# Two DMA queues in the sample attention, later splits, and prompt heads taken in pairs

## The reference, cut to what matters

```
c_kv = rmsnorm(kv[:256]);  k_rope = rope(rmsnorm(kv[256:]))       # 256-wide latent, 32-wide rotary key
kvb  = c_kv @ w_kv_b                                              # 16 heads x (64 key + 64 value)
k_nope = rmsnorm(kvb[..., :64]) ;  v = kvb[..., 64:]
s = (q_nope . k_nope + q_rope . k_rope) * 96**-0.5                # per head
p = softmax(where(k_pos//64 <= q_pos//64, s, -inf))
o = p @ v                                                         # then o @ w_o
```

## Time and profile before

| | us |
|---|---|
| median of 3 runs (1977.75 to 1983.08) | 1980.14 |
| the profiled execution, its own time | 1976.72 |
| its span | 1974.8 |

### The profile page before, as it was taken

One profiled execution on the slowest core, in us unless ns is written; L12 is line 12 of the kernel. 1 busy time (PEld: TensorE's weight loads), 2 busy tenths in 40 slices (PEclk: granted clock), 3 DMA queues, 4 the chain that ended last, 5 costly groups with the idle time before them and its releaser, 6 DMA issues.

```text
span 1974.8 us, 28317 instructions
## 1 busy us (share of the span) xinstructions
PE 1876.7 (95%) x10584; PEld 1765.5 (89%) x10584; DVE 1144.0 (58%) x1733; ACT 827.3 (42%) x1427; POOL 245.5 (12%) x315
## 2 busy tenths in 40 slices
PE   9999998999998999999999999999996799999997
PEld 8999998788887999999999999866775589999997
DVE  6555448778878655545855544456665555555444
ACT  5333335555464433334533333355453334333233
POOL 1000111220220000011300001140022222000020
PEclk9999999999999999999999999999998999999999
DMA  5444444455352544444344444421033433444441
GB/s 196 127 127 128 139 148 145 138 177 204 107 181 88 179 127 126 129 132 135 116 132 124 127 139 139 158 66 32 33 102 92 128 104 118 126 125 125 138 137 64
DMA packets 67779, 249.71 MB, mean 126 GB/s; under 512 B 9480, under 2 KB 10760, under 8 KB 66416
## 3 DMA queue, kind: packets, MB, share of 16 engines
q1 hardware_dynamic: 54000, 196.67, 32.4%
q0 software_dynamic: 13696, 51.90, 8.3%
HBM read 235.74 MB, written 12.12 MB: 126 GB/s over the span
## 4 chain that ended last, share of the span: by engine, by line
PE 81%; DVE 9%; ACT 5%; issue 2%; DMA 2%; POOL 1%; SPq 0%; ACTq 0%; DVEq 0%; POOLq 0%
PE pair L1753 23%; PE pair L1755 23%; PE pair L1754 23%; DMA kn<-rs_rows 2%; DVE wlo L1143 1%; PE pair L2169 1%; PE pair L1760 1%; PE pair L1762 1%; PE pair L1761 1%; PE pair L1950 1%; ACT kn L1012 1%; ACT seg L803 1%; PE pair L1969 1%; PE pair L2171 1%; PE pair L2170 1%
## 5 line engine op out<-in xcount | busy, mean ns | idle before, releaser
L1753 PE MATMUL pair<-xh,whi 128*128 128x384 f32 x1960 | 664.0, 339 | 14.8 <-DVE xl L1153 12.6
L1754 PE MATMUL pair<-xl,whi 128*128 128x384 f32 x1960 | 657.7, 336 | 0.0
L1755 PE MATMUL pair<-xh,wlo 128*128 128x384 f32 x1960 | 657.6, 336 | 0.0
L1143 DVE TENSOR_TENSOR wlo<-raw,whi 128x1024 fp32r<-128x1024 f32 (+3 forms) x372 | 463.1, 1246 | 181.3 <-ACT whi L674 172.5
L674 ACT ACTIVATE whi<-raw 128x1024 fp32r<-128x1024 f32 (+2 forms) x369 | 379.0, 1029 | 296.7 <-PE pair L1755 282.5
L1753 PEld LDWEIGHTS pair<-xh,whi 128*128 128x128 f32 x1960 | 370.3, 189 | 25.4 <-issue 14.2
L1754 PEld LDWEIGHTS pair<-xl,whi 128*128 128x128 f32 x1960 | 370.1, 189 | 1.8 <-issue 1.2
L1755 PEld LDWEIGHTS pair<-xh,wlo 128*128 128x128 f32 x1960 | 369.9, 189 | 0.0
L1163 DVE TENSOR_TENSOR tg<-pair,rstd 128x384 f32<-128x384 f32 x88 | 49.0, 557 | 331.2 <-PE pair L1755 330.6
L1753 PE MATMUL pair<-ah,whi 128*128 128x384 f32 x704 | 237.0, 337 | 3.5 <-DVE tu L1164 3.3
L1754 PE MATMUL pair<-al,whi 128*128 128x384 f32 x704 | 236.6, 336 | 0.0
(11 more groups left out here) (400 smaller groups left out, 2295.0 us busy)
## 6 DMA issues: line engine op xcount, KB each, us to landing
raw<-in_stream SPq DMA_DIRECT2D x372, 512.0 KB, 3.6
S<-in_ssm POOLq DMA_DIRECT2D x4, 2048.0 KB, 9.2
out_ssm_s<-S POOLq DMA_DIRECT2D x4, 2048.0 KB, 8.0
seg<-acs_rows POOLq DMA_DIRECT2D x12, 512.0 KB, 5.1
cTb<-in_cacheT POOLq DMA_DIRECT2D x10, 512.0 KB, 4.0
kn<-rs_rows POOLq DMA_DIRECT2D x16, 264.0 KB, 5.6
lowC<-in_cache POOLq DMA_DIRECT2D x8, 512.0 KB, 5.5
lowA<-in_cacheT POOLq DMA_DIRECT2D x6, 512.0 KB, 3.9
```

The lines of the kernel that those rows point to most:

```text
L1143: V.tensor_tensor(wlo[:, r, 0:w], raw[:, r, 0:w], whi[:, r, 0:w].bitcast(F32), ALU.subtract).then_inc(lo_ready, 1)
L1753: M(out, whi[:, r, ws], mh_(k), start=first and k == k0, stop=False)
L1754: M(out, whi[:, r, ws], ml_(k), start=False, stop=False)
L1755: ins = M(out, wlo[:, r, ws], mh_(k), start=False, stop=last and k == k1 - 1)
```

## The change

1. SP takes over the norm rows and the value transfers. Its weight loop is cut at block `WO + SLOTS`; between its two parts it issues `rstd_rows(u)` (the `kn` transfers) and `past_values(b)`, and POOL keeps the latent and rotary rows of the next stream.
2. `keys_split(b+2)` moves from even to odd u on ACT and DVE; on ACT it now stands ahead of `s_latent` and `s_exp(u+1)`. `keys_split(1)` stands ahead of `s_exp(0)` on ACT.
3. The prompt loop runs over 8 pairs y. Two score products, four expansions, six transposes in a row (bank 6 and bank 2), two expansions, six value products that alternate between the two heads, that is between the lower and upper half of the output partitions, then two expansions. `PT` has two slots. ACT and DVE are reordered to match; the low part of the next latent stands behind the pair's output.
4. Absorption uses banks 0, 1, 6, 7; the turn of the last key norms goes to bank 2 behind step 3, the first sample scores behind step 5.

```diff
-            with sp.Fori(1, NBLK // SLOTS) as i:
...
+            def rstd_rows(u):
+                if u >= 2:
+                    sp.wait_ge(s_added, u - 1)
+                sp.dma_start(kn[:, u % 2, 0:KEYS], rs_spread(u)).then_inc(rk_ld[u % 2], 16)
+            def past_values(b):
+                sp.wait_ge(po_ps, MH + 2 * max(b - 1, 0))
...
+            cut = WO + SLOTS
+            blocks(1, cut // SLOTS)
...
+            for u in range(2, UNITS):
...
+                rstd_rows(u)
+                if u % 2 and u >= 4:
+                    past_values(u // 2)
...
# POOL
-            for u in range(2, UNITS):
-                b = u // 2
...
-                past_rstd_rows(u)
-                if u % 2 == 0 and b + 2 < STREAMS:
-                    past_keys(b + 2)
-                    past_rope(b + 2)
-                if u % 2 and b >= 2:
-                    past_values(b)
+            for b in range(2, STREAMS):
+                past_keys(b)
+                past_rope(b)
# ACT, prompt loop
+            for y in range(MH // 2):
+                for i in range(3):
+                    past_square(8 * y + i)
+                p_turned(2 * y)
+                p_turned(2 * y + 1)
...
+                past_square(8 * y + 3)
+                if y + 1 < MH // 2:
+                    p_exp(2 * y + 2)
+                past_square(8 * y + 4)
+                if y + 1 < MH // 2:
+                    p_exp(2 * y + 3)
...
+                past_square(8 * y + 5)
+                act.wait_ge(po_ps, 2 * y + 2)
+                A(xh[:, y, 0:SEQ], bank[7 if y % 2 else 3][:, 0:SEQ], ACT.Copy).then_inc(oh_ready, 1)
+                if 2 <= y + 1 < STREAMS:
+                    past_split(y + 1)
+                past_square(8 * y + 6)
...
# ACT, sample loop
+            keys_split(1)
             s_exp(0)
-            keys_split(1)
             for u in range(UNITS):
+                if u % 2 and u // 2 + 2 < STREAMS:
+                    keys_split(u // 2 + 2)
                 if u >= 2:
                     s_latent(u - 2)
                 if u + 1 < UNITS:
                     s_exp(u + 1)
                 s_turned(u)
-                if u % 2 == 0 and 2 <= u // 2 + 2 < STREAMS:
-                    keys_split(u // 2 + 2)
# DVE, prompt loop
+                for i in range(8):
+                    past_sums(8 * y + i)
+                    if i == 2 and more:
+                        p_max(2 * y + 2)
+                    if i == 3 and more:
+                        p_max(2 * y + 3)
+                    if i == 5:
+                        if more:
+                            p_norm(2 * y + 2)
...
+                        if 2 <= y + 1 < STREAMS:
+                            past_split(y + 1)
+                    if i == 6 and more:
+                        p_norm(2 * y + 3)
# PE, prompt loop
+                for i in range(4):
+                    past_expand(8 * y + i)
...
+                for x in (2 * y, 2 * y + 1):
+                    pe.wait_ge(p_ready, x + 1)
+                    for j in range(3):
+                        ins = nc.tensor.transpose(bank[2 if x % 2 else 6][:, tiles(j)], Pb[:, x % 2, tiles(j)], ident[:, :])
+                    ins.then_inc(pt_ps, 1)
+                past_expand(8 * y + 4)
+                past_expand(8 * y + 5)
+                pe.wait_ge(pt_ev, 2 * y + 2)
...
+                for k, q, at in ((0, 0, 0), (0, 1, 1), (1, 1, 2)):
+                    for e in range(2):
+                        x = 2 * y + e
+                        ins = M(out[VH * e:VH * e + VH, tiles(q)], Vp[:, k, VH * x:VH * x + VH], PT[:, e, tiles(at)],
...
+                past_expand(8 * y + 6)
+                past_expand(8 * y + 7)
# PE, absorption
+            for j in range(4):
+                absorb(j)
+            pe.wait_ge(past_rstd, 4)
+            rs_turn(bank[2], 6, 8)
+            absorb(4)
+            absorb(5)
...
             s_scores(0)
+            absorb(6)
+            absorb(7)
```

More of the change, by code:

```diff
@@ L399, in build @@
         UNITS = 2 * STREAMS
+        QC_BANK = (0, 1, 6, 7)
         CRED = SLOTS
@@ L468, in _, with blocks, one_block @@
                 sp.dma_start(raw[:, r, :], T["stream"][r]).then_inc(raw_loaded[r], 16)
-            with sp.Fori(1, NBLK // SLOTS) as i:
-                for r in range(SLOTS):
-                    sp.wait_ge(lo_ready, i * SLOTS + (r - SLOTS + 1))
-                    sp.dma_start(raw[:, r, :], T["stream"][i * SLOTS + r]).then_inc(raw_loaded[r], 16)
+            def blocks(i0, i1):
+                with sp.Fori(i0, i1) as i:
+                    for r in range(SLOTS):
+                        sp.wait_ge(lo_ready, i * SLOTS + (r - SLOTS + 1))
+                        sp.dma_start(raw[:, r, :], T["stream"][i * SLOTS + r]).then_inc(raw_loaded[r], 16)
+            def one_block(n):
+                sp.wait_ge(lo_ready, n - SLOTS + 1)
+                sp.dma_start(raw[:, n % SLOTS, :], T["stream"][n]).then_inc(raw_loaded[n % SLOTS], 16)
+            def rstd_rows(u):
[4 more added lines that the diff above has]
+                sp.wait_ge(po_ps, MH + 2 * max(b - 1, 0))
+                sp.dma_start(cnat[:, b % 2], T["cache"][b]).then_inc(cn_ld[b % 2], 16)
+                sp.dma_start(vnew[0:STEPS, b % 2, :], ckv[STEPS * b:STEPS * b + STEPS, 2, :]).then_inc(cn_ld[b % 2], 16)
+            cut = WO + SLOTS
+            blocks(1, cut // SLOTS)
+            for n in range(cut // SLOTS * SLOTS, cut):
+                one_block(n)
+            sp.wait_ge(rs_st, 16 * 3)
+            sp.wait_ge(past_sum, 8 * STREAMS)
+            rstd_rows(0)
+            rstd_rows(1)
+            sp.wait_ge(filled, 6)
+            past_values(0)
+            past_values(1)
+            for u in range(2, UNITS):
+                if u == 12:
+                    sp.wait_ge(rs_st, 16 * 5)
+                rstd_rows(u)
+                if u % 2 and u >= 4:
+                    past_values(u // 2)
+            for n in range(cut, -(-cut // SLOTS) * SLOTS):
+                one_block(n)
+            blocks(-(-cut // SLOTS), NBLK // SLOTS)
         @block.gpsimd
@@ L1022, in _, with p_turned @@
             past_split(1)
+            def p_turned(x):
+                act.wait_ge(pt_ps, x + 1)
+                A(PT[:, x % 2, :], bank[2 if x % 2 else 6][:, 0:384], ACT.Copy).then_inc(pt_ev, 1)
             p_exp(0)
[L1024 to L1042, removed]
+            p_exp(1)
+            for y in range(MH // 2):
[3 more added lines that the diff above has]
+                p_turned(2 * y + 1)
+                if y == 0:
+                    A(rsT2[0:MH, P:2 * P], bank[2][0:MH, 384:512], ACT.Copy).then_inc(rs_ev, 1)
+                past_square(8 * y + 3)
[4 more added lines that the diff above has]
+                    p_exp(2 * y + 3)
+                else:
                     act.wait_ge(rs_turn_ps, 2)
@@ L1045, in _ @@
                     A(rsT2[0:6 * MH, 0:P], bank[2][0:6 * MH, 3 * P:4 * P], ACT.Copy).then_inc(rs_ev, 1)
[L1046 to L1052, removed]
+                past_square(8 * y + 5)
[4 more added lines that the diff above has]
+                past_square(8 * y + 6)
+                if y in (1, 2):
+                    z = (xh, xl)[y - 1]
+                    act.wait_ge(q_kept, 12)
+                    A(z[NOPE:QD, :, SEQ:TOK], Qs[NOPE:QD, 4 * y - 4:4 * y, :, :].rearrange("p b h q -> p (b h q)").rearrange(
+                        "p (k c) -> p k c", k=KD), ACT.Copy).then_inc(stack_hi, 1)
+                past_square(8 * y + 7)
+                if y == MH // 2 - 2:
+                    act.wait_ge(past_sum, 48)
+                    A(ksq[:, :, 0:6], ksq[:, :, 0:6], ACT.Sqrt, bias=EPS, scale=1.0 / NOPE).then_inc(past_std, 1)
             def keys_split(b):
@@ L1652, in _, with p_norm @@
             dve.wait_ge(mask_ld, 16)
-            p_max(0)
-            for x in range(MH):
+            def p_norm(x):
                 s, o = x % 2, 48 + 8 * (x % 2)
-                if x + 1 < MH:
-                    p_max(x + 1)
                 dve.wait_ge(p_exp_ready, x + 1)
@@ L1661, in _ @@
                 V.tensor_scalar(Pb[:, s, 128:384], Pb[:, s, 128:384], sm[:, o + 7:o + 8], None, ALU.mult).then_inc(p_ready, 1)
[L1662 to L1666, removed]
+            p_max(0)
+            p_max(1)
+            p_norm(0)
+            p_norm(1)
+            for y in range(MH // 2):
+                more = y + 1 < MH // 2
+                for i in range(8):
[7 more added lines that the diff above has]
+                            p_norm(2 * y + 2)
+                        dve.wait_ge(oh_ready, y + 1)
+                        V.tensor_tensor(xl[:, y, 0:SEQ], bank[7 if y % 2 else 3][:, 0:SEQ], xh[:, y, 0:SEQ].bitcast(F32),
+                                        ALU.subtract).then_inc(ol_ready, 1)
+                        if 2 <= y + 1 < STREAMS:
+                            past_split(y + 1)
+                    if i == 6 and more:
+                        p_norm(2 * y + 3)
```

(34 more changed lines are left out.)

58 lines of the change are left out of this document (14 added, 44 removed).

## The result

The changed kernel takes 1929.39 us (median, 1928.1 to 1929.83), the kernel before beside it 1981.61; the ratio is 0.9739, interval 0.9719 to 0.976. The prediction was 1932. The profiled execution took 1929.40 with a span of 1927.6.

The account below looks back on a forecast made before the run. It took PE to bound the prompt loop nearly fully and a ring over DVE, POOL and a DMA the sample loop. Gains 15.1 + 1.1 + 1.6 + 1.9 + 28.2 = 47.9 us gave 1932; own range 1923 to 1941, whole 1919 to 1953.

Parts of the forecast that it names:

- The bound of the sample loop: Units 1 to 13: without late transfers DVE's 8.97 us per two units; 9.6 taken, 28.2 us gained.
- the same ring: Sample loop: a ring over DVE, POOL and a DMA bound it, 14.3 us for a stream's two units.
- The prompt loop: Prompt heads: a pair takes 14.95 us in place of 16.84, 15.1 us gained, bounds 0 to 17.
- The restart of 0.27 behind transposes: Prompt loop: the first expansion behind a transpose takes 0.50, a restart of 0.27 us; the change drops one.
- Side by side: Rival, prompt loop: value products of different halves overlap, 6.4 us more gained, 1926 us; chance 0.15.
- the forecast's serial term (1.46): Prompt loop: a pair's six value products run one after the other, 0.80 us a head less a slow start of 0.14.
- Landings take over: Rival, sample loop: late `craw` or rotary rows make a pair landing + 3.1, 16.2 us gained, 1944 us; chance 0.18.
- The prompt ring: Rival, prompt loop: the chain overshoots its 0.5 us of room, a pair takes 16.4, 1944 us; chance 0.12.
- the slower rival: Rival, sample loop: SP serves norm rows slowly; at a landing of 20 us, 23.5 lost, 2004 us; chance 0.03.
- the third sign: Prompt loop: the forecast is wrong if PE waits for `past_lo` at the start of a pair; no size given.
- The entry: Way into the sample loop: 1.1 us gained before absorption, 1.6 from there to unit 0, 1.9 to unit 1.
- The untouched code: Rest of the kernel, outside the prompt loop, entry and sample loop: 0 us gained.

Follow-up runs that it names:

- e2: Kernel before with only the norm rows and value transfers moved to SP, splits still at even units: 1968.91 us, ratio 0.9925.
- e3: Kernel before with only the splits moved to odd units and the first ahead of the first exponential, transfers still on POOL: 1991.95 us, ratio 1.0043.
- e11: Changed kernel with a pair's six transposes taken apart (three, an expansion, three, an expansion): 1925.35 us.
- e1: Changed kernel with the six value products of a pair issued head by head, not alternating: 1931.08 us.
- e9: Changed kernel measured once more, unchanged: 1920.2 us, ratio 0.9699.
- the two together: Kernel before with both the SP queue move and the split move, prompt loop and absorption as before: 1951.8 us, ratio 0.9848.

## Why the prediction was right, and where it was off

**The bound of the sample loop** was named rightly. Taking the norm rows off POOL removed the transfers from the chain, and the next bound was DVE's own sum: forecast 8.97 for two units and 9.6 with late landings, measured 8.84 without a wait and 9.3 on average. Landings of the latent rose from 3.9 to a median of 5.2, inside the 5 to 6.5 assumed, and at most 7.5, over it; `craw` was what came next. e2 and e3 settle the mechanism: each had its size forecast from the same ring, and each came within 0.6 us of two units.

**The prompt loop** was forecast at 14.95 a pair and took 14.1; this is the mis-sized term, in three pieces. Its gain is also past the bound of 17 us that I called "all waits gone": the stretch gained 20.9, of which the wait ahead of the first absorption (1.79, then 0.78) gave 1.0. The restart of 0.27 behind transposes does not exist: the piece is 0.23 in the kernel after, and e11, with transposes in threes, has the same length of a pair. In the earlier trace rows the piece of 0.50 followed a wait for a square, and both views of the kernel before mark it, the chain in the piece ahead and the timeline behind the instruction:

```profile
1399.68 0.49 ACT kn L1012
...
1400.22 0.50 PE L2169 MATMUL pair<-wkh,cTh 128*128 128x512 f32 x1 [0.30 <-ACT kn L1012]
```

A piece that follows another engine's counts a matmul from its start to its end, where a piece behind PE's own counts only what it adds. The value products cost 0.81, not 1.46. Against that, a head's scores cost 0.65, not 0.47 (1.30 against 0.94 a pair): I had read them as the distance of two starts in the earlier trace rows, and part of their cost shows one place later, as 0.43 from the first start of the expansion behind them to the second, in place of 0.23. Net 14.73 - 0.27 - 0.65 + 0.36 = 14.17. The 0.22 that I added for collisions did not come.

**Side by side** was the rival I gave 0.15. Its mechanism is right, since six products cost what three did; the forecast's serial term (1.46) was wrong, and its own sign of being wrong, value products closer than 0.22, came: the records start 0.01 and 0.10 apart. e1 shows that only 0.26 of the 0.65 a pair depends on the alternation. The Trainium skill ("TensorEngine Tiling (Array Packing)", Key Properties: tiles operate independently) agrees with 0.81 for six.

**Landings take over** came in part, and with it another of the signs of being wrong: ACT waits for `craw` three times, 5.6 us in all. The two longest landings obey the rival's formula, landing + 3.1: 7.47 with a pair of 10.60, and 6.37 with one of 9.49. All such pairs together cost 2.9 us over six of 8.84, which the forecast's 9.6 had allowed for.

**The prompt ring and the slower rival** did not come as such: PE waits for `past_lo`, the third sign, at the last pair (0.93 us) and 0.3 us are lost in the pair of 14.47; `kn` costs DVE 1.1 us in all. The Trainium skill's rule on how many engines a transfer takes ("DMA: Bandwidth & Descriptors", "Why a DMA increments its semaphore by 16 and not by 1") is not tested, as no view here shows single engines; its outcome, landings near 8.5 us, did not appear.

**The entry** was right to 0.4 us in each of its three terms (1.0, 2.0 and 2.1 gained, 1.1, 1.6 and 1.9 forecast), though in the kernel before part of its 14.1 was half clock (0.76 over the first seven us), which I had not read.

**The untouched code** was costed at nothing and cost 7.9 us in the profiled run, and nothing in e9's. Without that loss the forecast is 12 us too high against e9's 1920.2, outside its own range of 1923 to 1941 and 1.2 us inside the whole one of 1919 to 1953. That the prediction came so close to 1929 is partly luck: the gain of the prompt loop that it missed and a clock that it could not foresee cancelled.

## What to carry to other kernels

When an in-order queue carries a transfer that is needed now behind one that waits for a later event, draw the ring and see where each edit cuts it: here, by the ratios, one edit alone gave 15 us, the other alone cost 9, and the two together gave 30. Before a piece of a chain is called a restart, check that the piece ahead of it isn't a wait; the same operation elsewhere in the trace without that neighbour tells. Before alternation is credited with an overlap, look at the starts of single records: part of it can be there in the old order. And compare two traces at common events before comparing totals, or a clock that fell elsewhere is read into the change.

## What was not expected of the hardware

Value products that write different halves of the output partitions cost 0.81 us for six, where three into one half cost 0.80. The granted clock behind the same wait near 356 us comes back within some 4 us or only after some 20, in the same file, and its runs fall into two kinds, 7 to 9 us apart, of 1920. What decides between the two stayed open.
